# Head gates as 24 more moving columns of a value product, and key blocks in the first phase

## The reference

```python
u = rms_norm(h, norm1_g[layer]) * (1 + scale1) + shift1
z = u @ w_in[layer]
q_a, kc, vc, ksl, vsl, kwn, vwn, g_a, q_b, k_b, v_b, m_a, m_b = jnp.split(z, split_at, axis=-1)
...
k_slc = rms_norm(ksl.reshape(kv_shape), k_norm_g[layer, 1])
k_win = rms_norm(kwn.reshape(kv_shape), k_norm_g[layer, 2])
g_nsa = jax.nn.sigmoid(g_a).reshape(B, S, NSA_KV_HEADS, NSA_GROUP, 3)
```

## Time and profile before

| what | value |
|---|---|
| median of three runs | 1047.05 us |
| profiled execution, its span | 1048.2 us (no time besides its span is given) |
| TensorE busy | 1026.5 us, 98% |
| VectorE busy | 804.9 us, 77% |
| ScalarE busy | 615.5 us, 59% |
| HBM read | 205.14 MB, 199 GB/s over the span |

### The profile page before, as it was taken

The page is one execution under the profiler, slowest core; times in us unless marked ns, Lnnn a source line. Parts: engine busy times, 40 slices in busy tenths (PEclk is TensorE's granted clock), DMA queues, the critical chain, the costliest instruction groups (busy, mean ns, idle before and its releaser), DMA issues.

```text
span 1048.2 us, 18924 instructions
## 1 busy us (share of the span) xinstructions
PE 1026.5 (98%) x6894; PEld 933.6 (89%) x6894; DVE 804.9 (77%) x1478; ACT 615.5 (59%) x1145; POOL 49.0 (5%) x74
## 2 busy tenths in 40 slices
PE   6999999999999999999999999999999999999998
PEld 5998989998988888988888889899999998888887
DVE  6987988877988655498887868567777868888753
ACT  5478789445656445466564457695654466565532
POOL 1011100011100000000000010000000020000000
PEclk8999999999999999999999999999999999999999
DMA  9997755666866666566665555545444555666663
GB/s 363 397 352 279 244 196 172 202 223 216 311 206 185 191 190 186 173 196 188 191 191 186 180 178 162 160 146 163 135 121 142 162 161 184 195 185 192 189 186 116
DMA packets 58508, 209.46 MB, mean 200 GB/s; under 512 B 7056, under 2 KB 8464, under 8 KB 57913
## 3 DMA queue, kind: packets, MB, share of 16 engines
q1 hardware_dynamic: 52616, 185.24, 55.5%
q0 software_dynamic: 5808, 23.09, 6.3%
HBM read 205.14 MB, written 3.16 MB: 199 GB/s over the span
## 4 chain that ended last, share of the span: by engine, by line
PE 88%; DVE 7%; ACT 3%; DMA 1%; issue 1%; DVEq 0%; ACTq 0%; SPq 0%
PE bank L691 87%; DVE ring_rounded L1856 3%; ACT rounded_rounded L1406 1%; PE bank L1038 1%; DMA ring<-in_stream 1%; DMA x<-in_x_t 0%; DVE ada_ring L2175 0%; DVE ada_ring L1912 0%; DVE body L1893 0%; ACT u_rounded L1463 0%; DVE body L2084 0%; DVE body_rounded L1900 0%; ACT body L1565 0%; DVE kcat L1986 0%; DVE part L2408 0%
## 5 line engine op out<-in xcount | busy, mean ns | idle before, releaser
L691 PE MATMUL bank<-u_rounded,rounded_rounded 128*128 128x256 f32 (+1 forms) x2152 | 508.8, 329 | 3.8 <-DVE ring_rounded L1856 3.4
L1856 DVE TENSOR_TENSOR ring_rounded<-ring,rounded_rounded 128x1024 fp32r<-128x1024 f32 x326 | 396.9, 1225 | 121.7 <-ACT rounded_rounded L1406 109.4
L1406 ACT ACTIVATE rounded_rounded<-ring 128x1024 fp32r<-128x1024 f32 x326 | 342.0, 1054 | 110.6 <-PE bank L691 90.7
L691 PE MATMUL bank<-u_rounded,ring_rounded 128*128 128x256 f32 x1504 | 352.3, 282 | 0.0
L691 PEld LDWEIGHTS bank<-u_rounded,rounded_rounded 128*128 128x128 f32 x2152 | 334.8, 189 | 7.6 <-issue 4.2
L691 PE MATMUL bank<-body_rounded,rounded_rounded 128*128 128x256 f32 (+1 forms) x1296 | 322.3, 336 | 2.0 <-DVE body_rounded L2114 1.3
L691 PEld LDWEIGHTS bank<-u_rounded,ring_rounded 128*128 128x128 f32 x1504 | 284.4, 189 | 36.8
L691 PE MATMUL bank<-body_rounded,ring_rounded 128*128 128x256 f32 x952 | 217.5, 281 | 0.0
L691 PEld LDWEIGHTS bank<-body_rounded,rounded_rounded 128*128 128x128 f32 x1296 | 201.7, 189 | 4.1 <-DVE body_rounded L2114 1.7
L691 PEld LDWEIGHTS bank<-body_rounded,ring_rounded 128*128 128x128 f32 x952 | 179.1, 188 | 26.3
L1660 ACT ACTIVATE part<-bank 128x256 f32<-128x256 f32 x65 | 24.9, 383 | 79.2 <-PE bank L691 79.2
(11 more groups left out here) (269 smaller groups left out, 883.8 us busy)
## 6 DMA issues: line engine op xcount, KB each, us to landing
ring<-in_stream SPq DMA_DIRECT2D x328, 512.0 KB, 4.1
ada_ring<-in_ada POOLq DMA_DIRECT2D x32, 512.0 KB, 5.7
body<-in_ada SPq DMA_DIRECT2D x8, 512.0 KB, 8.5
ada_ring<-in_ada SPq DMA_DIRECT2D x6, 512.0 KB, 7.6
mem_parts_kept<-body_rounded POOLq DMA_DIRECT2D x2, 1024.0 KB, 5.7
body_rounded<-mem_parts_kept POOLq DMA_DIRECT2D x2, 1024.0 KB, 5.4
x<-in_x_t SPq DMA_DIRECT2D x2, 512.0 KB, 4.6
body<-in_mem_t SPq DMA_DIRECT2D x2, 512.0 KB, 6.2
```

The costliest lines, as they stand in the source:

```text
L691: return nc.tensor.matmul(out, lhs, rhs, start=start, stop=stop, skip_group_check=True)
L1406: a(R(slot_round(q)), slot_weights(n), ACT.Copy).then_inc(slot_rounded, 1)
L1856: v.tensor_tensor(R(w), w, R(slot_round(q)), ALU.subtract).then_inc(slot_split, 1)
```

## The change

1. In the first phase the keys ks and kw take the places of vs and vw: two blocks with stationary weights and 256 moving tokens, both in bank 2.
2. vs, vw and the 24 gate columns become one product with tokens stationary and 280 columns moving, `project_packed`. Its weights are packed on the host, three steps of 280 columns in a slot of 1024, so that eight steps fill three slots (16 to 18), as many as ga, ks and kw had. Its outputs keep the names vsw0 and vsw1 and stand in banks 0 and 1 (`AFTER_FIRST`). The memory's sum goes to its middle.
3. The gates now arrive with tokens on the partitions, so `ga_turn` goes. ScalarE copies them out of the bank with the values, and takes the tanh in SBUF.
4. ga, ks, kw and ga_turn leave `proj_names`. qa0, qa2 and qa3 still get banks 0, 1 and 2, now right after vsw0, vsw1 and the keys. ma1 and ma2 go from bank 0 to bank 2, both.
5. ScalarE's copies out of vsw move behind `row_inv("mem_ss")`, and the calls of `ahead` are named after kc.

```diff
-FIRST_BANKS = {"vsb0": 0, "vsb1": 1, "vsw0": 2, "vsw1": 2, "kc": 3, "vc": 3, "kb0": 4, "kb1": 4, "kb2": 5, "kb3": 5,
+FIRST_BANKS = {"vsb0": 0, "vsb1": 1, "ks": 2, "kw": 2, "kc": 3, "vc": 3, "kb0": 4, "kb1": 4, "kb2": 5, "kb3": 5,
...
+AFTER_FIRST = {"vsw0": 0, "vsw1": 1}
...
-        for c in (C_VS, C_VW, *(C_VB + j * P for j in range(4)), C_KC, C_VC):
+        for c in (C_KS, C_KW, *(C_VB + j * P for j in range(4)), C_KC, C_VC):
...
-    stationary("w_in", span(C_GA), full)
-    for c in (C_KS, C_KW):
-        stationary("w_in", span(c), full)
+    for j in range(-(-KD // PACK) * SLOT):
+        out.append(("values_and_gates", j, None))
...
+            def project_packed(names, k, lhs, halfway):
+
+                ps = [claim(n) for n in names]
+                hi, lo = lhs
+                for i in range(k):
+                    if i == k // 2:
+                        halfway()
+                    if i % PACK == 0:
+                        chunk = at["chunk"]
+                        w_hi, w_lo = take(SLOT)
+                    c = slice(i % PACK * PACKED, (i % PACK + 1) * PACKED)
+                    for t in range(TT):
+                        at_t = slice(t * P, (t + 1) * P)
+                        ins = mm(ps[t][:, 0:PACKED], R(hi[:, i, at_t]), w_hi[:, c], i == 0)
+                        if t == 0 and i % PACK == 0:
+                            give_back(ins, chunk)
+                        mm(ps[t][:, 0:PACKED], R(hi[:, i, at_t]), w_lo[:, c])
+                        ins = mm(ps[t][:, 0:PACKED], R(lo[:, i, at_t]), w_hi[:, c], stop=i == k - 1)
+                        if i == k - 1:
+                            done(ins, names[t])
...
-            project("ga", KD, u_parts)
-            project("ks", KD, u_parts)
-            ps = claim("mem_ss")
-            pe.wait_ge(mem_summed, 3)
-            done(mm(ps[:, 0:T], mat("ones"), mem_squares[:, 0, :], True, True), "mem_ss")
-            project("kw", KD, u_parts)
+            project_packed(("vsw0", "vsw1"), KD, u_parts, sum_memory)
...
-                evacuated(pe, "ga")
-                ps = claim("ga_turn")
-                for t in range(TT):
-                    ins = mm(ps[:, t * 24:(t + 1) * 24], gate_raw[:, t * P:(t + 1) * P], mats[0:24, MAT["ident"], 0:24], t == 0, t == TT - 1)
-                done(ins, "ga_turn")
...
             for t in range(TT):
-                output(f"vsw{t}")
-            for t in range(TT):
-                src = bank(f"vsw{t}")[:, t * T:(t + 1) * T].rearrange("p (r s d) -> p r s d", r=2, d=HD)
-                a(vcat[:, t, :, 0, 0:HD], src[:, :, 0, :], ACT.Copy)
-                free(a(vcat[:, t, :, 1, HD:P], src[:, :, 1, :], ACT.Copy), f"vsw{t}")
-            for t in range(TT):
                 spread_heads(pair_v[:, t, :, :], f"vsb{t}")
+            ahead("kc", 5)
             for w, n in enumerate(("kc", "vc")):
...
-            copy(gate_raw, "ga", bank("ga")[0:24, 0:T])
             key_blocks(0)
+            ahead("kc", 6)
             square("ks")
-            row_inv("mem_ss")
-            square("kw")
+            square("kw", T)
             key_blocks(2)
+            ahead("kc", 7)
+            row_inv("mem_ss", 1)
+            for t in range(TT):
+                output(f"vsw{t}", 3)
+                src = bank(f"vsw{t}")[:, 0:T].rearrange("p (r s d) -> p r s d", r=2, d=HD)
+                a(vcat[:, t, :, 0, 0:HD], src[:, :, 0, :], ACT.Copy)
+                a(vcat[:, t, :, 1, HD:P], src[:, :, 1, :], ACT.Copy)
+                free(a(gate_tanh[:, t, :], bank(f"vsw{t}")[:, T:T + GA], ACT.Copy), f"vsw{t}")
```

More of the change, by code:

```diff
@@ L43 @@
 SLOT = 8
+GA = 24
+PACKED = 2 * P + GA
+PACK = SLOT * P // PACKED
 RAW_GATES = 4
@@ L261, in plan_psum @@
     where, used = {}, [0] * 8
-    for name, b in [*BEFORE_FIRST.items(), *FIRST_BANKS.items()]:
+    for name, b in [*BEFORE_FIRST.items(), *FIRST_BANKS.items(), *AFTER_FIRST.items()]:
         where[name] = (b, used[b])
@@ L286, in proj_names @@
 def proj_names():
-    out = ["ga", "ks", "kw", "qa0", "qa2", "qa3"]
+    out = ["qa0", "qa2", "qa3"]
     out += ["cmp_hid_k", "cmp_hid_v", "ma0", "cmp_turn_k", "cmp_turn_v"]
-    out += ["ga_turn", "ma1", "cmp_out_k", "cmp_out_v", "ma2", "ma3", "ma4"]
+    out += ["ma1", "cmp_out_k", "cmp_out_v", "ma2", "ma3", "ma4"]
     return out
@@ L456, in build @@
         table = sb("table", [33, 8])
-        gate_tanh = sb("gate_tanh", [P, TT, 24])
+        gate_tanh = sb("gate_tanh", [P, TT, GA])
         gate_t = sb("gate_t", [P, 8, 6])
@@ L476, in build @@
         kc_windows = kc_ext.rearrange("p w h t -> p w (h t)")
-        gate_raw = turned[0:24, 1, 1, 0:T]
         row_squares = turned[:, :, :, :].rearrange("p a b c -> p (a b c)").rearrange("p (k t) -> p k t", t=T)
@@ L864, in _ @@
             done(mm(claim("bias")[0:8, 0:512], table[:, :], buckets[:, :], True, True), "bias")
-            first = {n: bank(n)[:, T:2 * T] if n in ("vsw1", "vc", "kb1", "kb3", "qb1", "qb3") else
+            first = {n: bank(n)[:, T:2 * T] if n in ("kw", "vc", "kb1", "kb3", "qb1", "qb3") else
                      bank(n)[:, 0:512 if n in ("vsb0", "vsb1") else T] for n in FIRST_BANKS}
             def opens(name):
-                return name in ("vsb0", "vsb1", "vsw0", "kc", "kb0", "kb2", "qb0", "qb2")
+                return name in ("vsb0", "vsb1", "ks", "kc", "kb0", "kb2", "qb0", "qb2")
             def first_tokens(names, k, w_hi, w_lo):
@@ L1416, in taken, with square @@
                 evacuated(act, name)
-            def square(name):
+            def square(name, first=0):
                 n = n_squares[0]
@@ L1421, in square @@
                 output(name)
-                a(squares[:, n % SQ, :], bank(name)[:, 0:T], ACT.Square).then_inc(squares_ready, 1)
+                a(squares[:, n % SQ, :], bank(name)[:, first:first + T], ACT.Square).then_inc(squares_ready, 1)
             def inv_rms(name, width, last_reader):
@@ L1585, in _ @@
                         ins.then_inc(cmp_tanh_ready, 1)
-                    output("ga_turn", HALVES - 1)
-                    free(a(gate_tanh[:, :, :], bank("ga_turn")[:, 0:48].rearrange("p (t g) -> p t g", t=TT), ACT.Tanh, scale=0.5), "ga_turn")
+                    for t in range(TT):
+                        evacuated(act, f"vsw{t}")
+                    a(gate_tanh[:, :, :], gate_tanh[:, :, :], ACT.Tanh, scale=0.5).then_inc(gate_tanh_ready, 1)
                     nc.scalar.preload_act_table_set("natural_log_exp_and_others")
@@ L1970, in _ @@
             for b in range(4):
-                ahead("vsw0", 3 + b // 2)
+                ahead("kc", 3 + b // 2)
                 full(dve, f"qb{b}")
@@ L1982, in key_norms @@
                 r = take_rinv()
-                late = 272 + off
+                late, at = 272 + off, 0 if n == "ks" else T
                 for s, rr in enumerate((LO, HI)):
                     for first, dst in ((0, off), (P, late)):
-                        ins = v.scalar_tensor_tensor(out=kcat[rr, s, dst:dst + P], in0=bank(n)[rr, first:first + P],
+                        ins = v.scalar_tensor_tensor(out=kcat[rr, s, dst:dst + P], in0=bank(n)[rr, at + first:at + first + P],
                                                      scalar=col("k_slc_norm" if n == "ks" else "k_win_norm", 0, rr),
@@ L2490, in lay_out @@
         src[n] = np.concatenate([pairs[0::2], pairs[1::2]], axis=2)
+    packed = np.zeros((-(-KD // PACK), P, SLOT * P), np.float32)
+    for k in range(KD):
+        w = sq["w_in"][k * P:(k + 1) * P]
+        packed[k // PACK, :, k % PACK * PACKED:(k % PACK + 1) * PACKED] = np.concatenate(
+            [w[:, C_VS:C_VS + P], w[:, C_VW:C_VW + P], w[:, C_GA:C_GA + GA]], axis=1)
+    src["values_and_gates"] = packed.reshape(-1, P, SLOT, P).transpose(0, 2, 1, 3).reshape(-1, P, P)
     chunks = stream_chunks()
```

22 lines of the change are left out of this document (12 added, 10 removed).

## The result

The changed kernel is slower: 1052.72 us median of 10 runs (1049.13 to 1055.94) against 1047.98 of 10 runs of the kernel before (1045.40 to 1051.78). The ratio of the two is 1.0040, with a 95% interval of 1.0026 to 1.0054, so the change costs 4.2 us by the ratio (2.7 to 5.7) and 4.7 by the medians. The forecast was 1052.0, a difference of 5.0. The same two kernels timed again gave 1051.39 (6 runs) against 1047.59, ratio 1.0035 (1.0021 to 1.0050), 3.7 us by the ratio.

The account below looks back on a forecast made before the run. TensorE was taken as the bound, with DMA engines also full. qa0 late 4.8 plus clock 1.7 less 1.5 absorbed gives 5.0; 1047.05 + 5.0 = 1052.0 us, narrow forecast 1050.5 to 1053.3, range 1048.2 to 1054.0.

Parts of the forecast that it names:

- The saving: TensorE's projections after the first phase: 72 products of 256 columns become 48 of 280, saving 2.39 us, all inside the stall.
- ScalarE's list: Slot 18's rounding now precedes kc's and vc's copies; ScalarE idles 5.2 us, bank 0 frees at 78.2, qa0 starts 4.8 late.
- The landing: Slot 18's transfer, issued at 56.22, ends ScalarE's wait at 66.56, 10.3 us later, as in the kernel before.
- Rival A: No loss or gain if slot 18 lands by 61.4; each microsecond later than 62.7 costs qa0 one; 1047.0 us, chance 0.10.
- The clock: After almost 7 us of TensorE idling before qa0, the lower clock loses 1.7 us; bounds 0 and 2.5.
- VectorE's floor: VectorE starts the memory's normalising 4.0 us late and works without real gap to qa2's, so cmp_hid_v is at least 4.0 late.
- The absorbed 1.5: TensorE's wait before cmp_hid_v for VectorE's normalising of qa2 absorbs up to 1.5 us of the delay.
- The turned gates: Two removed products, at most 0.59 us of TensorE at 97.57, worth nothing since ma2 waits for ScalarE's copy of ma1.
- No giving back: From cmp_hid_v on, TensorE waits only for work it set off itself, so the delay of 5.0 us reaches the end.
- B: Rival: the whole saving arrives, 1044.7 us, or 1044.1 with the gates' products; chance 0.02 together with E, a list not as described.
- C: Rival: transfers land 1 to 2 us earlier or clock stays up; 1051.0 with clock alone, 1049.3 with both; chance 0.18.
- D: Rival: lower clock holds 6 us or more and VectorE's chain falls behind too; 1054.5 us, chance 0.10.

Follow-up runs that it names:

- e1: Changed kernel with ScalarE's rounding of slot 18 put back behind the copies of kc and vc; 1048.01 us, ratio to before 1.0004.
- e6: Changed kernel, slot 18's rounding behind kc, vc, kb0, kb1; vsw's copies before slot 20's rounding; VectorE splits slot 20 inside the memory's normalising; 1048.33 us, ratio 1.0008.
- e7: As e6, with two of VectorE's ada steps moved from between qa's normalisings to around the first softplus; 1046.32 us, ratio to before 0.9987.
- e8: As e7, with the 1 MB attention bias load issued later, as in e3; 1045.82 us, ratio to before 0.9982.
- e3: Changed kernel with the 1 MB attention bias load issued behind five parameter loads on GpSimd's queue instead of three; 1051.07 us, ratio to before 1.0029.
- e5: The changed kernel run again unchanged; 1051.39 us (6 runs), 3.8 us above before by the medians.
- e9: Changed kernel with two fp32 products of 256 columns added behind cmp_turn, standing for the turned gates; one profiled run, no comparison of times.
- e4: Changed kernel with 20 thrown-away products of 256 columns filling TensorE's idle time before qa0; 1049.51 us, ratio to before 1.0017.
- e2: Changed kernel with vsw0 and vsw1 copied out right behind the squares, slot 18's rounding still in front; 1051.84 us, ratio to before 1.0034.

## Why the prediction held, step by step

- **The saving.** 0.128 us for a product of 280 columns, forecast 0.130: 72 x 0.120 less 48 x 0.128 are 2.5 us of TensorE's time, forecast 2.39. How much of it arrives depends on the other lists. In the medians: nothing in e1 and e6, 1.3 to 1.8 us in e7 and e8. In the stretch: 1.2 in e1, 2.5 in e8, where TensorE waits 0.71 us before qa0 and 0.37 before cmp_hid_k, less than before's 1.5 in the same stretch. e1's median has nothing of its 1.2 (the interval is -0.8 to +1.8 us against before). In its profiled execution 0.7 of it is lost again behind the stretch (955.9 against 955.2 us); the rest stays open.
- **ScalarE's list.** Right in order and durations (8 copies 3.12 us, forecast 3.14; from slot 18's start to bank 0 free 76.43 - 64.96 = 11.5, forecast 78.2 - 66.56 = 11.6). e1 shows that it is the cause.
- **The landing.** The one input that did not repeat. Rival A's sentence, that each microsecond of it costs qa0 one, holds: from e3 to e5 the landing moves by 3.0 us and qa0 by 3.0. The forecast of 5.0, moved to each execution's own landing and with its own clock loss in place of 1.7 (qa0's time less 3.06), gives: after 5.0 - 1.9 - 0.5 = 2.6 (measured 2.7), e5 5.0 - 0.2 + 0.2 = 5.0 (5.1), e9 5.0 - 0.8 + 0.5 = 4.7 (4.8), e3 5.0 - 3.2 - 0.4 = 1.4 (1.5). It is one rule with four landings. The table says the same without the forecast: from slot 18 to the end, less the time of qa0, lie 26.80, 26.77, 26.78 and 26.81 us in after, e3, e5 and e9, so nothing but the landing and the clock tells them apart.
- **The clock.** Forecast 1.7; qa0 took 1.2, 1.3, 1.9 and 2.2 us more than before's 3.06 in after, e3, e5 and e9. With the idle time filled (e4) or 1.9 us at most (e1, e2, e6, e7, e8) nothing is lost. The runs without a profile agree: the mean granted clock is 0.9946 and 0.9945 in the ten and six runs of the kernel after, 0.9967 and 0.9970 in the 35 and 29 of before. Over 1050 us this is 2.2 to 2.6 us of TensorE's full clock. Part of it falls into idle time: in after, e3, e5 and e9 the stretch from 70 to 84 lacks 1.7 to 3.4 us of it, and qa0 lost 55 to 78% of that. So the clock costs 1.2 to 2.0 us in the medians, an estimate from these figures.
- **VectorE's floor.** e2 shows it (4.0 less the 3.2 us of its earlier landing and with the 0.8 of row_inv's later place are 1.6, measured 1.4), and e4: its 2.5 us late is the floor of 4.0 less the 1.3 us by which slot 18 landed earlier, 2.7.
- **The absorbed 1.5.** The wait at cmp_hid_v is gone in after, e3, e5 and e9.
- **The turned gates.** Worth nothing, as e9 shows.
- **No giving back.** 955.2 and 955.1 us from there to the end, where the clock falls near 256 us in both. In e5 it doesn't, and that execution is 1.5 us shorter behind the stretch. I had not reckoned with this; it is no effect of the delay, since e2, e7 and e8 have it too, early and late.

Of the rivals, B is excluded by every profile. A and C are not other theories but the same one at an earlier landing: the profiled execution of after is 2.7 us late, which lies between C's two figures (1051.0 and 1049.3, 4.0 and 2.2 above 1047.05). The mechanism is shown, and the nearness of the number, 5.0 against 4.7, is partly luck. The forecast rests on a landing 2.52 us behind F, the latest that any profile here has. In the five executions whose lists up to that rounding are those of the kernel after (after, e2, e4, e5, e9) it came 0.65, -0.65, 1.19, 2.33 and 1.74 behind F, 1.05 in the mean. By the rule above that makes 3.5 us (an estimate), against 4.2 and 3.7 by the two ratios; the difference is inside their intervals. So the time was right with its range, but the chance of 0.60 for the narrow forecast was more than one execution's landing could bear. (Half of C's 0.18 is 0.09, so the chance of slower by more adds up to 0.79 and not 0.78.)

D, the lower clock for 6 us or more, came in part: in e5 the windows from 72 to 84 add up to 6.8 us at the lower level (a granted clock of 0.79 and 0.64), but some of that passed while TensorE stood idle. qa0 lost 1.9 us, in e9 2.2, and the result stayed under D's time.

Why slot 18 lands when it does is not shown. It goes with the head start of GpSimd's loads, and e3 moved only the last of them; the time did not tell it from the kernel after. A run that moves the three in front of it would settle it.

## What to carry to other kernels

Where an engine takes its list in order, an operation that waits for a transfer is put behind everything that is ready, not in front of it: here one rounding moved ahead of eight copies, which were ready before its data, cost 3.8 us by the ratios (4.7 by the medians) where the change saved 2.5. Work taken from the bounding engine is only worth what the engines that free its banks and make its operands can keep up with: move their lists with it (e8's edits here gave 1.8 us of 2.5), and look for the next wait by the profile after each. Freeing a bank earlier is worth nothing when the operand behind it comes from a chain that is just as late.
